# Expert tiles of 104 rows, one fixed overflow tile, and a down product in two parts of each operand

## The reference, cut to what matters

```
x = x + concat(o_a, o_b, o_c) @ w_out
h = rmsnorm(x)
grp = argmax(h @ w_grp + b_grp)                  # 4 groups
top_val, top_idx = top_k(logits of the 8 experts of grp, 2)
for e in range(32):
    out = out + (silu(h @ w_gate[e]) * (h @ w_up[e]) * gate[:, e]) @ w_down[e]
```

## Time and profile before

| | us |
|---|---|
| median of 3 runs | 1219.35 (1219.16 to 1222.54) |
| profiled execution | 1231.86 |
| span of its instructions | 1230.1 |
| PE busy | 1107.8 (90%) |
| DVE busy | 596.7 (49%) |
| ACT busy | 382.3 (31%) |
| POOL busy | 211.4 (17%) |

### The profile page before, as it was taken

How to read it: one execution, slowest core, us unless ns; L and a number is a source line. 1 busy time by engine, 2 the same in 40 slices (tenths; PEclk the granted TensorE clock), 3 DMA queues, 4 the chain that set the end, 5 groups by cost and what they waited for, 6 DMA issues and landing times.

```text
span 1230.1 us, 29634 instructions
## 1 busy us (share of the span) xinstructions
PE 1107.8 (90%) x12090; PEld 903.3 (73%) x12090; DVE 596.7 (49%) x1584; ACT 382.3 (31%) x693; POOL 211.4 (17%) x460
## 2 busy tenths in 40 slices
PE   5999899999899999999899899948999999999910
PEld 5989788778688888888777688847777777776700
DVE  5341344225466666665685434464344433333428
ACT  6411112222355555544677122200111111111103
POOL 1020000000333233221374000010001000000040
PEclk9999899999799999999999899967999999999965
DMA  9021744362557878764321422277999999999464
GB/s 350 18 86 37 271 149 151 139 187 98 126 113 182 208 204 219 196 147 95 106 62 28 155 95 96 79 279 260 379 378 376 406 374 369 387 384 371 188 238 198
DMA packets 69430, 251.59 MB, mean 205 GB/s; under 512 B 22224, under 2 KB 30320, under 8 KB 59440
## 3 DMA queue, kind: packets, MB, share of 16 engines
q1 hardware_dynamic: 59376, 219.54, 53.5%
q0 software_dynamic: 6112, 16.79, 4.0%
q10 hardware_dynamic: 3808, 13.37, 2.9%
HBM read 205.34 MB, written 49.15 MB: 207 GB/s over the span
## 4 chain that ended last, share of the span: by engine, by line
PE 72%; DMA 12%; DVE 7%; issue 4%; SPq 2%; ACT 1%; POOL 1%; DVEq 1%; POOLq 0%; ACTq 0%
PE PS L2145 13%; PE PS L1826 12%; PE PS L2002 8%; PE PS L2153 8%; PE PS L2082 8%; PE PS L1815 5%; DMA wdn<-in_wdn 5%; PE PS L1980 4%; PE PS L1941 3%; PE PS L1981 3%; DMA k<-T_d 3%; PE PS L2136 2%; DVE x L1772 1%; SPq L620 1%; DMA wst<-in_wt 1%
## 5 line engine op out<-in xcount | busy, mean ns | idle before, releaser
L2145 PEld LDWEIGHTS PS<-XT,wgu 128*64 128x64 f32 x4352 | 185.3, 139 | 31.6 <-issue 30.6
L1088 ACT ACTIVATE pt<-PS,cst 128x512 f32<-128x512 f32 (+3 forms) x288 | 168.0, 652 | 115.4 <-PE PS L1981 88.2
L2145 PE MATMUL PS<-XT,wgu 128*64 128x96 f32 x4352 | 191.4, 250 | 5.8 <-issue 2.7
L1396 DVE CUSTOM_DVE_ANT_0 junkm<-PS,cst 128x512 f32<-128x512 f32 (+3 forms) x276 | 133.5, 531 | 86.9 <-PE PS L1941 85.1
L2002 PEld LDWEIGHTS PS<-V,pt 128*64 128x64 f32 x3840 | 122.4, 138 | 22.5 <-issue 9.5
L2002 PE MATMUL PS<-V,pt 128*64 128x65 f32 x3840 | 137.9, 226 | 0.1
L2153 PE MATMUL PS<-wdn,aT 128*96 128x512 f32 x272 | 122.7, 593 | 1.6 <-DVE YO L1720 0.9
L1826 PE MATMUL PS<-hTh,wth 128*128 128x512 f32 x256 | 102.9, 402 | 5.0 <-DVE wtl L1243 5.0
L1826 PE MATMUL PS<-hTh,wtl 128*128 128x512 f32 x256 | 100.7, 393 | 0.0
L1826 PE MATMUL PS<-hTl,wth 128*128 128x512 f32 x256 | 100.7, 393 | 0.0
L821 POOL TENSOR_SCALAR_AFFINE_SELECT pt<-pt 128x128 f32<-128x128 f32 x224 | 64.6, 294 | 164.4 <-ACT pt L1088 121.2
(11 more groups left out here) (275 smaller groups left out, 1630.9 us busy)
## 6 DMA issues: line engine op xcount, KB each, us to landing
wgu<-in_wgu SPq DMA_DIRECT2D x34, 2048.0 KB, 13.8
wdn<-in_wdn SPq DMA_DIRECT2D x34, 1024.0 KB, 21.1
q<-T_d SPq DMA_DIRECT2D x58, 256.0 KB, 4.2
k<-T_d SPq DMA_DIRECT2D x58, 256.0 KB, 5.4
Y_d<-YO ACTq DMA_DIRECT2D x34, 384.0 KB, 10.0
wst<-in_wt SPq DMA_DIRECT2D x16, 512.0 KB, 7.0
T_d<-thi SPq DMA_DIRECT2D x16, 512.0 KB, 2.6
T_d<-tlo SPq DMA_DIRECT2D x16, 512.0 KB, 3.9
```

The lines of the kernel that those rows point to most:

```text
L1088: ins = nc.scalar.activation(pt[:, (n + 2) % 6, 0:nt * P], PS[:, n % 3, 0:nt * P], ACT.Exp, scale=C("slopes", h, h + 1), bias=C("kb", w, w ...
L1396: V_.tensor_tensor_reduce(out=junk_[:, 0:L], in0=PS[:, bank, 0:L], in1=tab, scale=1.0, scalar=-3e38, op0=ALU.add, op1=ALU.max, accum_out=m ...
L2145: ins = mm(PS[h * HD:(h + 1) * HD, 2 + p, f * CAP:(f + 1) * CAP], wgu[q][:, c, lo:lo + HD], XT[:, p, c, :], start=(c == 0 and f == 0), sto ...
```

## The change

1. CAP is 104 in place of 96 and SURE is 1 in place of 2, so that NB is 33 in place of 34.
2. The down product of the fixed tiles takes high and low parts. ACT makes the high part of the weights (`wd_high`, two copies of 128x1024) and of the activations (`a_part`), DVE the low parts (`wd_low`, two subtractions of 128x1024, and `a_rest`), and PE does 12 products in f32r in place of 4 in f32. The high part of the weights has one buffer, in the place of a table that only attention reads.
3. The landings of `wgu` and `wdn` are counted apart: up(n) waits for `wgu` only, the copy of the high part for `wdn`.
4. SP waits for the first gathered tile before it loads the weights of tiles 2 and 3, and no longer before those of tile 4.
5. At the start of attention the queries and keys of `PLAN.full[2]` are counted by a semaphore of their own, on which its first pass for the maxima waits; the loads of `PLAN.full[3]` are issued behind the first shift row, and SP doesn't wait ahead of them.
6. The transposes of the first half for the output projection go ahead of the last slot's products with the values, `o_lo` of that half ahead of the last attention output on DVE, and PE's wait for `o_free` goes to the second token tile.

```diff
-CAP = 96
+CAP = 104
 MAX_OVF = 2 * SEQ // (CAP + 1)
-SURE = 2
+SURE = 1
...
+                ins.then_inc(lx_in if x is PLAN.full[2] and dst in (Q1, K1) else ld_in[x.set], 16)
...
             load_unit(PLAN.full[2])
             load_unit(PLAN.full[1])
-            sp_.wait_ge(ld_in[PLAN.full[2].set], 96)
-            load_unit(PLAN.full[3])
...
+                if f == 1:
+                    load_unit(PLAN.full[3])
...
             load_expert(1, 1)
+            sp_.wait_ge(xg_in[0], 16)
             load_expert(2, 2)
             sp_.wait_ge(h_lg, 8)
             load_expert(3, 3)
             sp_.wait_ge(dve_did, DV.of("ids_ov"))
-            sp_.wait_ge(xg_in[0], 16)
             load_expert(4, 4)
...
+            def wd_high(n):
+                act.wait_ge(wd_in[n % RING], 16 * (n // RING + 1))
+                if n:
+                    act.wait_ge(m_dn, n)
+                for c in range(2):
+                    copy(wdnh[:, c, :], wdn[n % RING][:, c, :]).then_inc(wd_hi, 1)
+
+            def a_part(n):
+                act.wait_ge(m_prod, n + 1)
+                if n >= 2:
+                    act.wait_ge(m_dn, n - 1)
+                copy(aTh[:, n % 2].rearrange("p c t -> p (c t)"), gd[:]).then_inc(m_ah, 1)
+
             m_x(0)
             for n in range(NB):
                 m_exp(n)
                 if n + 1 < NB:
                     m_x(n + 1)
+                a_part(n)
                 if n:
                     m_out(n - 1)
+                wd_high(n)
             m_out(NB - 1)
...
+            def a_rest(n):
+                flat_ = lambda x: x[:, n % 2].rearrange("p c t -> p (c t)")
+                dve.wait_ge(m_ah, n + 1)
+                V_.tensor_tensor(out=flat_(aTl), in0=gd[:], in1=flat_(aTh).bitcast(f32), op=ALU.subtract)\
                   .then_inc(m_act, 1)
+
+            def wd_low(n):
+                for c in range(2):
+                    dve.wait_ge(wd_hi, 2 * n + c + 1)
+                    V_.tensor_tensor(out=wdnl[n % RING][:, c, :], in0=wdn[n % RING][:, c, :],
+                                     in1=wdnh[:, c, :].bitcast(f32), op=ALU.subtract).then_inc(wd_lo, 1)
...
             for n in range(NB):
                 m_gate(n)
+                a_rest(n)
                 if n:
                     m_out(n - 1)
+                wd_low(n)
...
+                if slot_ == LAST:
+                    o_transposes(0, (0,))
+                for x, k in PLAN.s_at.get(slot_ - PLAN.DEEP, ()):
+                    values(x, k)
...
+                        for x, w in ((aTh, wdnh), (aTl, wdnh), (aTh, wdnl[q])):
+                            ins = mm(PS[0:CAP, 5 + h, :], x[:, p, c, :], w[:, c, h * 512:(h + 1) * 512],
+                                     start=(c == 0 and x is aTh and w is wdnh), stop=(c == 1 and w is wdnl[q]))
...
             def m_down(n):
                 pe_.wait_ge(m_act, n + 1)
+                pe_.wait_ge(wd_lo, 2 * n + 2)
```

More of the change, by code:

```diff
@@ L462, in program @@
         h_st = [sem(f"h_st{p}") for p in range(2)]
-        we_in = [sem(f"we_in{q}") for q in range(RING)]
+        wu_in = [sem(f"wu_in{q}") for q in range(RING)]
+        wd_in = [sem(f"wd_in{q}") for q in range(RING)]
+        wd_hi = sem("wd_hi")
+        wd_lo = sem("wd_lo")
+        m_prod = sem("m_prod")
+        m_ah = sem("m_ah")
         xg_zero = sem("xg_zero")
@@ L1505, in _, with o_lo @@
             t_lo(15, 1, (1,))
+            def o_lo(t, p, halves=(0, 1)):
+                for c in halves:
+                    dve.wait_ge(g_hi, 2 * t + c + 1)
+                    V_.tensor_tensor(out=otl[:, p, 4 * c:4 * c + 4, :].rearrange("p k t -> p (k t)"),
+                                     in0=PS[:, c, :],
+                                     in1=oth[:, p, 4 * c:4 * c + 4, :].rearrange("p k t -> p (k t)").bitcast(f32),
+                                     op=ALU.subtract).then_inc(g_lo, 1)
             for slot_ in SLOTS:
+                if slot_ == LAST + 1:
+                    o_lo(0, 0, (0,))
                 for x, c in PLAN.out_at.get(slot_, ()):
@@ L1928, in max_pass @@
                     pe_.wait_ge(ky_in, 32)
+                elif k == 0 and x is PLAN.full[2]:
+                    pe_.wait_ge(lx_in, 64)
                 elif k == 0 and x.kind != "C":
@@ L1960, in scores @@
                     pe_.wait_ge(aug_set[s], 2)
-                    if x.n == 2:
+                    if x in PLAN.full[1:3]:
                         pe_.wait_ge(ld_in[s], loaded(x))
@@ L2045, in o_transposes @@
                     ins.then_inc(g_tr, 1)
+            for slot_ in SLOTS:
+                for x, k in PLAN.s_at.get(slot_, ()):
+                    scores(x, k)
+                for x, k in PLAN.m_at.get(slot_, ()):
+                    max_pass(x, k)
+                for x in PLAN.tp_at.get(slot_, ()):
+                    shift_T(x)
+                if slot_ == LAST:
+                    o_transposes(0, (0,))
+                for x, k in PLAN.s_at.get(slot_ - PLAN.DEEP, ()):
+                    values(x, k)
             def h_transposes(t):
@@ L2152, in down_product, with down_plain @@
                     for c in range(2):
-                        ins = mm(PS[0:CAP, 5 + h, :], aT[:, p, c, :], wdn[q][:, c, h * 512:(h + 1) * 512],
+                        for x, w in ((aTh, wdnh), (aTl, wdnh), (aTh, wdnl[q])):
+                            ins = mm(PS[0:CAP, 5 + h, :], x[:, p, c, :], w[:, c, h * 512:(h + 1) * 512],
+                                     start=(c == 0 and x is aTh and w is wdnh), stop=(c == 1 and w is wdnl[q]))
+                return ins
+            def down_plain():
+                for h in range(2):
+                    for c in range(2):
+                        ins = mm(PS[0:CAP, 5 + h, :], aT[:, c, :], wdn[0][:, c, h * 512:(h + 1) * 512],
                                  start=(c == 0), stop=(c == 1))
```

65 lines of the change are left out of this document (28 added, 37 removed).

## The result

The kernel after takes 1228.2 us (median of 4, 1223.7 to 1231.8) beside 1219.7 us for the kernel before (median of 4): a ratio of 1.0055, 95% interval 1.0031 to 1.008. The forecast was 1199. In another session, with 12 and 29 executions, the ratio was 1.0014 (0.9992 to 1.0036). The change thus gains nothing, and by the ends of the two intervals it loses between nothing and 0.8 per cent.

The account below looks back on a forecast made before the run. The prediction took PE to bound the expert stage, with DMA right under it. Stage -10.3, start of attention -8.0, start of projection -2.2 and routing +0.1 made -20.4, from 1219.35 to 1199 us; range 1187 to 1213.

Parts of the forecast that it names:

- DMA per tile: Expert stage: eight more store rows, spread evenly, add 0.08 us, so the slowest engine needs 10.54 us per tile.
- Rival (b): Expert stage: 104 rows don't spread over 16 engines, some get eight; 11.15 us per tile, 1215.5 in all; chance 0.20.
- upper bound of my range, 11.15: Expert stage: DMA time per tile if some engine gets eight rows of the store and of each gather.
- When DMA binds: Expert stage: counting from tile 5's weights landing after 12.9 us, loads set the last up product's end, 1152.7 against 1166.67.
- PE alone: Expert stage: without waits for loads, at 9.47 us per tile, the last up product ends at 1144.3.
- Tail: Last expert tile: no up product hides the split, gather of Y_d comes at 16.7 us for 13.0, costing 3.7 us.
- The base: Whole kernel: sum made against the profiled 1231.86 us; the median's 12.5 us lower time taken over as it is.
- the starts: Start of attention gains 8.0 us (4.5 to 9.5), start of the output projection 2.2 us (1 to 2.8).
- 5.86, 2.78 and 9.50 us of PE: Expert tile on PE: up product 5.86 us, down product 2.75, whole tile 9.47, 0.21 less than now.
- the loop over DVE and ACT that just fits: Expert tile: DVE's queue is 9.4 us long in a tile of 9.47, so the split stays hidden.
- rival (c): Expert stage: the DVE and ACT loop becomes the bound; 10.43 us per tile loses all, 10.6 gives 1224; chance 0.07.
- the first gather: Front of the expert stage: it lands 4.5 us after issue, not 9.0; first up product 3.2 us gained, bounds 2 and 4.

Follow-up runs that it names:

- store2: The kernel after with each store to Y_d as two transfers, of 96 and of 8 rows: 1234.8 us, 1.0052 of the kernel before.
- early_loads: The kernel after with item 4 undone, weights of tiles 2 and 3 loaded without waiting for the first gathered tile: 1239.3 us, 1.0099 of before.
- after_again: The kernel after unchanged, timed and profiled again beside the kernel before: 1221.6 us, 1.0014 of before.
- after_skip: The kernel after with the loop for further overflow tiles inside a condition, so that no empty trip is made: 1219.7 us, 0.9994 of before.
- light_dma: after_skip with only half of the gate and up weights loaded from tile 5 on, output not the reference's: 1197.9 us, 0.981 of before.
- before_skip: The kernel before with the loop for further overflow tiles inside a condition, so that no empty trip is made: 1220.8 us, 0.999 of before.
- starts_skip: The kernel before with items 5 and 6 and the condition around the overflow loops (96 rows, 34 tiles, f32 down product): 1212.0 us, 0.9872 of before.
- split_starts_skip: starts_skip with items 2 and 3 too, the split down product on 96 rows and 34 tiles: 1212.2 us, 0.9874 of before.
- starts_gather: starts_skip with item 4 too, the first gather ahead of the weights of tiles 2 and 3: 1211.5 us, 0.9846 of before.
- tiles: The kernel before with item 1 alone (104 rows, 33 tiles): 1248.6 us, 1.0163 of before.
- after_skip2: after_skip once more, in the session where the kernel before takes 1229.6 us: 1220.8 us, 0.9931 of before.
- store96: after_skip with the store of each tile taking its first 96 rows only, output not the reference's: 1.0002 of before.

## Why the prediction was wrong

**DMA per tile: the term that was mis-sized.** I took 10.46 + 0.08 = 10.54, from "evenly spread". It measured 10.74, against 10.42 of before in the same way: 0.32 more, four times my term, and 0.2 x 27 = 5.4 us at the end of the stage. Rival (b) had the mechanism, the store. The Trainium skill (DMA: Bandwidth & Descriptors, "Why a DMA increments its semaphore by 16 and not by 1") has a rule that puts 104 rows on 13 engines. By it and the earlier trace rows the store adds 0.34, an estimate, and 0.23 to 0.29 was measured. The spread over engines is not in any row, so that the mechanism is borne out by the size and the mean share alone, and store2, which should have saved up to 0.17, saved 0.03 to 0.09. The upper bound of my range, 11.15, should have been 11.2 by its own terms (10.46 + 0.34 + 0.40), which moves rival (b) to 1217 and changes nothing else.

**When DMA binds: the start of the count.** The landing that I counted from, 12.9 us for tile 5, was that of the old order of loads. With tiles 2 and 3 behind the gather it was 19.6, from an issue 25.0 us behind the first up product, where I had 25.7: 44.6 us behind it for 38.6, 6.0 later. Not all of that is the order's: in early_loads, with the old order, the same landing takes 16.1 us and comes 42.5 us behind the first up product. Both together make the loads 11.3 us later at the last tile, and PE adds the 2.6 us by which it starts behind them; these are the 14 us that the stage takes more than predicted. PE first waited for `wgu` at tile 20, where I had said 24.

**A step that was missing: PE stops and a low clock beside busy DMA engines.** I let PE lose time by waits for weights alone, and had put anything else at nothing. The kernel after stops for 8.1 us (9.8 in after_again, 9.9 in after_skip) within products, the kernels with the f32 down product for 0.0 to 3.2, and light_dma for 0.0. How much of this reaches the end of the stage isn't shown, beyond the 2.6 us: a stop while PE waits for loads anyway costs nothing. And the longest wait costs twice: after the 2.31 us of waiting that end at 1107.93, the up product takes 7.55 for 5.86. The busy time from 1105 to 1116 us has the clock at 0.84; behind the shorter waits, of 0.7 to 1.7 us, it stayed full (1.00 from 870 to 1060 us):

```profile
1105.00:1116.00 11.00, 8.41 (x132) 7.68 (x130) 4.21 (x7) 2.86 (x4) 0.00 (x0) 0.84 0.99 346
```

PE alone, 315.3 by my sum, was right: 314.4 in light_dma.

**Tail.** +3.7 predicted, +6.3 found; the split's end was right, the clock of the last product (5.43 us for 2.75) was not in the sum. It is 2.6 of the 29.3 us.

**The base.** I took the 12.5 us between the profile of before and its median over as they were. They were in part slow trips of the empty loop: 17.5 us from the first branch that closes a trip (1176.3) to the last (1193.8), where trips at the 0.53 us of their beginning take 9.5.

```profile
L1731 DVEq COMPARE_BRANCH  x19: 7/56/712, 1176.3 to 1193.8; - x19
```

By the phase behind the last up product (63.4 us, 58.1 in before_skip) they make some 5 of the 12.5 us; another 4 lie ahead of the projection, whose first product starts at 682.5 for 678.75 in before_skip, and their cause stays open. The unprofiled executions had less to give. I had looked at the loop as work that makes no trip, and not counted that it comes after another store when the number of tiles turns odd.

**What was right:** the starts (8.9 measured in the time for 10.2, with an interval of 6 to 12), 5.86, 2.78 and 9.50 us of PE, the loop over DVE and ACT that just fits (rival (c) was not what made the kernel slower: light_dma has the same loop and tiles of 9.50 us to the end), the first gather.

**What stays open:** what makes the trips slow in some executions, and whether they are behind the level of a session; why the stops come with the split (12.7 us at 96 rows, too) and so little with f32, although the instruction packets are as many and the DMA engines as busy (share 1.01 and 1.01 from 870 to 1060 us in starts_skip and split_starts_skip); and how the last 2.6 us of the stage divide between stops and clock.

## What to carry to other kernels

When a second bound lies under the first, a faster engine buys nothing beyond the slack, and eight more rows in a transfer can cost more than their bytes: take its price from landing to landing over many tiles, and count from the landings of the new order. Before you take over the gap between a profile and the median, look for what in the profile could vary. And the last pass of a loop has nothing behind it to hide in: giving it the short form alone was worth 5 to 8 us, and with it the split on 96 rows beats both kernels (0.981). Most of that is the starts and the condition around the loop; beside starts_gather of the same session (0.9846), which has the f32 down product, it is 5 us.

## What the runs showed of the hardware

- Trips of a loop whose body is skipped take 0.53 us on DVE in the profiles of after and after_again; beside the gathers of `Y_d` some executions (tiles, early_loads, store2) take up to 2.8 us per trip, in steps of 0.7 us per branch or register instruction, on DVE, ACT and SP at once.
- Beside DMA engines that are full (share 0.99 to 1.01), PE stopped in the middle of a product for up to 2.7 us (after_skip2), each time 1.2 to 1.7 us behind a packet of the instruction queue; at a share of 0.86 (light_dma) it didn't stop.
- 104 rows for 96 made the weights land 0.3 us later per tile (10.74 us in after, 10.42 in before); with a store of 96 rows it was 10.48 (store96).
- Around a wait of 2.3 us on PE and the up product behind it the clock granted was 0.84 over 11 us, and the product took 7.55 us for 5.86; after 6 us without work, twelve products took 5.43 us for 2.78, at 0.57.
